# A fused transformer kernel in fp32: tiled score and compression matmuls, squares added on VectorE, a split GLU, and sparse attention ahead of latent attention

## The chip, the core and the metric

One core of one Trainium2 chip runs the whole program in one launch. The metric is device microseconds from the start to the end of an execution; the number compared is the median over several executions. The engines are named as in the profile: PE (TensorE matmul), PEld (its weight loads), DVE (VectorE), ACT (ScalarE), POOL (GpSimd) and SP (SyncE, which issues the weight loads from memory).

## The reference, cut to what matters

256 tokens of width 1024 go through one block of a first kind and then two layers of a second kind, all in fp32.

```python
def first_block(x, ...):
    xn = rms_norm(h, ln1_g)
    u_s5, q, k, v, gate_logits = split(xn @ w_in)
    y_s5 = s5_mixer(u_s5, ...) @ w_s5_branch      # scan, gelu, then ab = y @ w_glu; a * sigmoid(b)
    y_attn = sliding_window_attention(q, k, v, ...) @ w_attn_branch
    h = h + (g_s5 * y_s5 + g_attn * y_attn) @ w_out
    xn2 = rms_norm(h, ln2_g)
    return h + peer_mixer(xn2, w_query, sub_keys, u, v)   # s = q . sub_keys, top 16, 16384 experts

def layer(h):                                     # twice
    xn = rms_norm(h, attn_norm)
    q, k_cmp, v_cmp, k_sel, v_sel, k_win, v_win, gates, c_q, c_kv, k_rope = split(xn @ w_in)
    # NSA: compressed keys and values by a small MLP over blocks of 32 tokens (silu(flat @ w1) @ w2),
    # softmax over 15 compressed blocks, over the selected blocks and over the window; gated sum
    # MLA: q and k from normed c_q, c_kv; rotary part; softmax; values from c_kv
    h = h + concat(rms_norm(nsa), rms_norm(mla)) @ w_out
    xn = rms_norm(h, mlp_norm)
    return h + relu(xn @ w_ff1) ** 2 @ w_ff2
# at the end: rms_norm(h, final_norm)
```

## The kernel before, in words

Everything lies transposed: features on the 128 partitions, the 256 tokens along the free axis, so h is 8 chunks of 128x256. Weights come in units of 128x1024 fp32 (512 KB) in the order of use, through a ring of four SBUF slots that SP fills (L163 to L175, `Ring.load`).

**Split products.** Most products are made of three passes of fp32r matmuls: high part of the weights times high and low part of the data, low part of the weights times the high part. For each unit ACT rounds the weights to their high part (L177 to L185, `Ring.round`; two buffers `wh`, the next round waits until PE has finished the unit two before) and POOL subtracts to get the low part (L192 to L200, `Ring.subtract`). A slot is loaded again when POOL has made the low part (`rest`). `split_pair` (L1894) and `pair_product` (L516) take two units of 24 matmuls of 128x256 each. Other products are unsplit fp32 matmuls, which the trace records as two records each, and their slot comes free when PE has used it: `linear_part` (L364), `compress` (L2074), the scores (L1979), the sums of squares (L331 and L1883).

**PSUM** has 8 banks. `Banks.plan` (L95) gives each job its bank and its place in the order on that bank, by hand; `open` waits on PE until the job before it on the bank is drained, `take` waits on the reader until the job is full.

**The order of work on each engine is written out by hand**, an instruction stream per engine (`first_pe`, `first_act`, `first_dve`, and `layers_pe`, `layers_act`, `layers_dve`). Each engine takes its stream strictly in order; the position of a `ring.round` in ACT's stream is part of that order.

**The stretches of the program**, by the profile's times: the first block up to its last product (0 to 278.9 us) with the GLU inside (197.4 to 226.0), the two row products of the 16384 experts (to 1065), and twice a layer, made of its attention part (1068.9 to 1236.2 and 1429.0 to 1597.3) and its feed-forward part; the end is 1790.2 to 1804.0.

- In the first block PE makes `u` 0, then the sum of the squares of h by a matrix of ones over 8 chunks (L1173, L336), then `u` 1. ACT's stream is there: round, the eight high parts, round, the squares (L641), round, `table(0)` (sine and cosine tables, which wait for DVE's `angles(0)`, L827), round, the root of the mean square (L650).
- The GLU (L1245 to L1252) makes gb, ga and ys by 8 unsplit units.
- After `pq` (L1257 to L1261) and the first two expert rows, PE makes the 8 key score jobs of the experts (L2418 to L2426): 16 matmuls of 128x256 whose keys are padded with zeros to 128 rows. They use 4 banks, drained by ACT at L2243.
- In a layer PE does: cq, sum of 8 squares, ckr, q0, sum, turn, q1, the latent queries uq and keys uk and values uv (unsplit), the rotations rk and rq, kvc, latent scores (t = 0), rp, kk, latent scores (t = 1), rc, rp2, V, `compress` of the values (16 matmuls with 30 weight columns, L2080), the scores of the selected branch, `compress` of the keys, the scores of the window branch, then transposes and outputs of the latent heads, compressed scores sc, sum of 4 squares, the branch products wm, then (after a wait for the window probabilities and the compressed ones) transposes and outputs of the NSA heads, sum of 4 squares, branch products wn, and the feed-forward part with one more sum of 8 squares (mf). The keys KZ2 of the NSA scores are padded with zeros to 128 rows.
- DVE writes the scores with mask to SBUF (L1729), takes the row maximum (L1733, `row_max`), ACT makes the exponentials with their sums (L1552), DVE scales them by the reciprocal of the sum (L1742, `probabilities`). Rotations (`rope`, L1701) are PE, then three DVE instructions. The compressed scores are scaled, masked, shifted, normed in SBUF (L1807 to L1832).
- The end (L2192): sum of 8 squares after all four squares (L1646), root, reciprocal, scaling, store.

## Time and profile before

| | us |
|---|---|
| median of 3 executions | 1812.35 (1809.46 to 1813.52) |
| profiled execution, its own time | 1806.09 |
| its span in the profile | 1804.0 |
| mean granted TensorE clock | 0.987 of 2.4 GHz |
| PE busy / DVE / ACT / POOL | 95% / 49% / 51% / 66% |

The span is from the first to the last instruction of the profiled execution; 2.1 us of its own time lie outside. Busy time of PE counts a matmul from its start to its modelled end, so neighbours overlap: what one matmul costs in a row of equal ones is read from start to start. A fp32 matmul has two records.

### The profile page before, as it was taken

Reading aid. Unit: us, or ns where it says so; the run is one execution under the profiler, and the core shown is the slowest. Engines: PE = TensorE matmul, PEld = TensorE weight load, DVE = VectorE, ACT = ScalarE, POOL = GpSimd, SP = SyncE. Lnnn points to the kernel's source line nnn. Section 1 sums busy time; section 2 is a strip of 40 time slices with the busy share of each in tenths; the row PEclk is TensorE's granted clock in tenths of the full one; section 3 lists DMA queues with packets and bytes.
Section 4 is the critical chain, followed back from the end, with each engine's and each line's share of the span. In section 5 each row is a group of like instructions: output and inputs, shape, how many; then the busy total and the mean of one; then the engine's idle time right before and its main releaser. Section 6 shows DMA issues by size and latency. Waiting matters only on the chain.

```text
span 1804.0 us, 31918 instructions
## 1 busy us (share of the span) xinstructions
PE 1706.8 (95%) x12716; PEld 1545.4 (86%) x12716; DVE 875.9 (49%) x1854; ACT 912.1 (51%) x1530; POOL 1186.9 (66%) x492
## 2 busy tenths in 40 slices
PE   7988999989999999999999999988999989889997
PEld 7886899989999997777788887678999976789997
DVE  6978336991266666777511124853210148532101
ACT  5566355444544444555566664564653444646532
POOL 5552277898777776777788874215888741158885
PEclk9989999999999999999999999999999999899999
DMA  7332554655555554555566644413556543135563
GB/s 239 127 117 60 173 167 153 190 150 181 169 166 167 168 167 152 167 173 167 183 195 194 193 153 149 133 44 108 185 186 187 166 141 129 46 107 186 187 187 106
DMA packets 79603, 280.42 MB, mean 155 GB/s; under 512 B 8672, under 2 KB 9440, under 8 KB 79200
## 3 DMA queue, kind: packets, MB, share of 16 engines
q1 hardware_dynamic: 79456, 278.38, 49.3%
q8 instruction: 101, 1.65, 0.4%
q14 instruction: 46, 0.38, 0.1%
HBM read 277.30 MB, written 1.05 MB: 154 GB/s over the span
## 4 chain that ended last, share of the span: by engine, by line
PE 63%; DVE 5%; ACT 2%; issue 2%; POOL 1%; POOLq 0%; DVEq 0%; ACTq 0%
PE ps L2471 13%; PE ps L1903 13%; PE ps L2173 9%; PE ps L2478 6%; PE ps L2451 4%; PE ps L2452 3%; PE ps L2456 3%; ACT attention L1552 1%; POOL wl L199 1%; DVE attention L1729 1%; PE ps L1889 1%; PE ps L2437 1%; PE ps L1959 1%; PE ps L2439 1%; PE ps L2080 1%
## 5 line engine op out<-in xcount | busy, mean ns | idle before, releaser
L199 POOL TENSOR_TENSOR wl<-slots,wh 128x1024 fp32r<-128x1024 f32 x228 | 546.8, 2402 | 448.7 <-ACT wh L184 441.4
L2276 POOL TENSOR_TENSOR wl<-slots,wh 128x1024 fp32r<-128x1024 f32 x256 | 635.3, 2485 | 150.9 <-ACT wh L2216 148.8
L2216 ACT ACTIVATE wh<-slots 128x1024 fp32r<-128x1024 f32 x256 | 271.3, 1060 | 391.5 <-issue 234.3
L184 ACT ACTIVATE wh<-slots 128x1024 fp32r<-128x1024 f32 x228 | 240.5, 1060 | 263.0 <-PE ps L2173 105.5
L2451 PE MATMUL ps<-xh,wh 128*128 128x256 f32 x1024 | 255.9, 288 | 0.9 <-ACT small L2252 0.9
L2452 PE MATMUL ps<-xl,wh 128*128 128x256 f32 x1024 | 250.4, 282 | 0.0
L2451 PEld LDWEIGHTS ps<-xh,wh 128*128 128x128 f32 x1024 | 195.4, 191 | 1.1 <-ACT small L2252 1.1
L2452 PEld LDWEIGHTS ps<-xl,wh 128*128 128x128 f32 x1024 | 195.9, 191 | 0.0
L2471 PE MATMUL ps<-wh,xh 128*128 128x512 f32 x512 | 164.5, 403 | 4.4 <-DVE xl L2390 4.4
L2471 PE MATMUL ps<-wh,xl 128*128 128x512 f32 x512 | 160.0, 394 | 0.0
L2456 PE MATMUL ps<-xh,wl 128*128 128x256 f32 x1024 | 144.3, 284 | 7.9 <-POOL wl L2276 7.8
L2456 PEld LDWEIGHTS ps<-xh,wl 128*128 128x128 f32 x1024 | 131.9, 192 | 9.7 <-POOL wl L2276 9.7
L2478 PE MATMUL ps<-wl,xh 128*128 128x512 f32 x512 | 137.6, 391 | 0.0
L2173 PE MATMUL ps<-hidden_hi,wh 128*128 128x256 f32 x512 | 124.3, 280 | 1.9 <-POOL wl L199 1.9
L2390 DVE TENSOR_TENSOR xl<-ps,xh 128x256 fp32r<-128x256 f32 x128 | 53.7, 419 | 145.2 <-ACT xh L2231 145.2
L2173 PE MATMUL ps<-hidden_lo,wh 128*128 128x256 f32 x512 | 124.0, 279 | 0.0
L2478 PEld LDWEIGHTS ps<-wl,xh 128*128 128x128 f32 x512 | 96.4, 188 | 21.4
L2471 PEld LDWEIGHTS ps<-wh,xl 128*128 128x128 f32 x512 | 96.6, 189 | 21.0
L1903 PE MATMUL ps<-xh,wh 128*128 128x256 f32 x704 | 106.7, 291 | 6.9 <-ACT wh L184 4.6
L2383 DVE SCALAR_TENSOR_TENSOR arena<-ps,arena 128x256 f32<-128x256 f32 x128 | 54.4, 425 | 118.6 <-PE ps L2439 118.6
L2471 PEld LDWEIGHTS ps<-wh,xh 128*128 128x128 f32 x512 | 91.6, 189 | 20.6 <-issue 4.6
L1903 PEld LDWEIGHTS ps<-xh,wh 128*128 128x128 f32 x704 | 93.0, 193 | 13.6 <-issue 8.2
(357 smaller groups left out, 3204.6 us busy)
## 6 DMA issues: line engine op xcount, KB each, us to landing
slots<-w SPq DMA_DIRECT2D x260, 512.0 KB, 3.5
slots<-wu SPq DMA_DIRECT2D x128, 512.0 KB, 3.5
slots<-wv SPq DMA_DIRECT2D x128, 512.0 KB, 3.5
arena<-bias SPq DMA_DIRECT2D x1, 2048.0 KB, 8.1
h<-xT SPq DMA_DIRECT2D x2, 512.0 KB, 5.5
...
yT<-y_out SPq DMA_DIRECT2D x2, 512.0 KB, 2.6
...
```

Of the source, the lines that this page charges most:

```text
L184: act.activation(self.hi[:, n % 2, :], self.slots[:, u % SLOTS, :], ACT.Copy).then_inc(self.rounded, 1)
L199: pool.tensor_tensor(self.lo[:, n % 2, :], self.slots[:, self.order[n] % SLOTS, :], self.hi[:, n % 2, :].bitcast(F32), ALU.subtract).then_ ...
L1903: ins = pe.matmul(halves[j], w[:, k, :], x[:, k, :], start=(first and k == 0), stop=(last and k == DC - 1), skip_group_check=True)
L2173: return pe.matmul(out_banks[c // 2][:, (c % 2) * T:(c % 2 + 1) * T], w[:, c * P:(c + 1) * P], x[:, u, :], start=start, stop=False, skip_g ...
L2216: act.activation(whv[:, r % 2, :], slots_v[:, r % SLOTS, :], ACT.Copy).then_inc(w_hi, 1)
L2276: pool.tensor_tensor(wlv[:, r % 2, :], slots_v[:, r % SLOTS, :], whv[:, r % 2, :].bitcast(F32), ALU.subtract).then_inc(w_lo, 1)
L2383: dve.scalar_tensor_tensor(a, grid, 1.0 / GATE_SCALE, a, ALU.mult, ALU.mult).then_inc(g_done, 1)
L2451: pe.matmul(out, hi[:, k, :], xhT[:, k, :], start=(k == 0), stop=False)
L2452: ins = pe.matmul(out, hi[:, k, :], xlT[:, k, :], start=False, stop=False)
L2456: ins = pe.matmul(out, lo[:, k, :], xhT[:, k, :], start=False, stop=(k == DC - 1))
L2471: ins = pe.matmul(psum[2 * t + half], part_a[:, tokens], hi[:, half * 512:(half + 1) * 512], start=begins, stop=False, skip_group_check=True)
L2478: ins = pe.matmul(psum[2 * t + half], a_hi[:, t * P:(t + 1) * P], lo[:, half * 512:(half + 1) * 512], start=False, stop=(row == NE2 - 1), ...
```

## The change

What it does, part by part:

- **Added squares.** `add_squares` adds the chunks of squares on DVE (a reduction over a strided view), so that PE sums one matmul for each group of chunks: 1 for 8 in the first block (ms), 2 for 8 in ms2, ms and mf, 1 for 4 in mm and mn. At the end the 8 chunks stay, each pair awaited by itself.
- **Split GLU.** gb, ga and ys become split products (`split_linear`); ACT makes u_hi and glu_hi and rounds 8 more units, POOL subtracts 8 more, DVE makes u_lo and glu_lo.
- **Tiled key scores** of the experts: 32 matmuls of 64 rows and 128 columns, in pairs on the two row halves, two banks open at a time.
- **Tiled NSA scores**, in the same manner: for each group and t 8 matmuls of 64 rows in 4 pairs in place of 4 of 128 rows and twice the columns.
- **Tiled compression**: four matmuls with 32 weight columns each side by side in the four column groups, then ACT copies the 128 rows, and one more matmul by a matrix that adds the four tiles (`add_tiles`).
- **Compressed scores in PSUM**: their chain on DVE and ACT works in the bank of sc; only the finished probabilities go to SBUF.
- **The order of a layer**: rotations behind each product, NSA first, latent attention after it, wn before wm; the order of loads, rounds and banks with it. The NSA transposes use 3 banks in place of 7, the latent scores 2 in place of 4.

```diff
+        def add_squares(dve, squares, slot, signal):
+            dve.tensor_reduce(added[:, slot, :], squares.rearrange("p c t -> p t c"), AX.X, ALU.add).then_inc(signal, 1)
...
+        u_hi, u_lo, glu_hi, glu_lo = mix_hi[:, 0:4], mix_hi[:, 4:8], mix_lo[:, 0:4], mix_lo[:, 4:8]
...
@@ first_act, after the Gelu activations
+            act.wait_ge(s_gelu, UC)
+            act.activation(u_hi, uT, ACT.Copy).then_inc(s_uhi, 1)
+            ring.round(act, 2)
             for i in range(2):
                 b = banks.take(act, ("gb", i))
                 banks.give(act.activation(sig[:, 2 * i:2 * i + 2, :], two(b[:, :]), ACT.Sigmoid), ("gb", i))
+                ring.round(act, 1)
+            for i in range(2):
+                act.wait_ge(s_glu, i + 1)
+                b = banks.tensors[banks.jobs[("ga", i)][0]]
+                act.activation(glu_hi[:, 2 * i:2 * i + 2, :], two(b[:, :]), ACT.Copy).then_inc(s_ghi, 1)
+                ring.round(act, 1)
+            ring.round(act, 2)
...
@@ first_dve, ahead of angles(0)
+            dve.wait_ge(s_sq, 1)
+            add_squares(dve, sq, 0, s_pre)
             dve.wait_ge(loaded_c, 16)
             angles(0, early(0))
...
-            sum_squares(pe, "ms", sq, DC, (s_sq, 1))
+            sum_squares(pe, "ms", added, 1, (s_pre, 1))
...
-                    linear_part(pe, (name, i), ring.unit(pe).rearrange("p (k n) -> p k n", k=4), uT, (0, P))
+                    split_linear((name, i), u_hi, u_lo, lambda: pe.wait_ge(s_ulo, 1))
...
-            sum_squares(pe, "ms2", sq4, DC, (s_sq4, 4))
+            sum_squares(pe, "ms2", added, 2, (s_pre, 3))
...
@@ layers_act, from the root of msn on
+                copy(("kk", l), raw_k)
                 ring.round(act, 2)
                 b = banks.take(act, ("kvc", l))
                 act.activation(raw_c[:, 0, :], b[:, 0:T], ACT.Copy).then_inc(l_raw, 1)
                 ring.round(act, 1)
+                copy(("q", l, 1), raw_q[:, 2:4, :])
+                ring.round(act, 2)
+                copy(("cv", l), hidden_rows[:, 1, :])
+                exponentials(0, SELECTED, 0)
...
+                copy(("ck", l), hidden_rows[:, 0, :])
+                exponentials(0, SELECTED, 1)
...
+                for i in range(2):
+                    copy(("uq", l, i), qMr[:, 2 * i:2 * i + 2, :])
+                exponentials(1, WINDOW, 0)
...
+                for t in range(TT):
+                    copy(("uv", l, t), Vm[:, t, :])
+                exponentials(1, WINDOW, 1)
...
                 ring.round(act, 2)
...
+                exponentials(2, MLA, 0)
+                exponentials(2, MLA, 1, range(4))
+                ring.round(act, 1)
+                exponentials(2, MLA, 1, range(4, 8))
+                ring.round(act, 1)
+                banks.give(take_root(("mn", l), 512, root[:, 0:T]), ("mn", l))
                 transposed(16)
                 transposed(17)
...
@@ layers_dve
+                rope(("rp", l, 0), raw_q[:, 0:2, :], cos_r, sinr, add_to(qA[:, 0:2, :]))
                 banks.give(two_shifts(1, b[:, T:2 * T], rst[:, 0:T], ALU.mult), ("kvc", l))
                 windows(1)
                 rope(("rp", l, 2), raw_k, cos_r, sinr, split_keys)
+                rope(("rp", l, 1), raw_q[:, 2:4, :], cos_r, sinr, add_to(qA[:, 2:4, :]))
+                row_max(SELECTED, 0)
+                rope(("rc", l), raw_c, cos_r, sinr, lambda x, y: two_shifts(0, x[:, 0, :], y[:, 0, :], ALU.add))
+                windows(0)
+                row_max(SELECTED, 1)
+                projected_keys(0)
+                projected_keys(1)
+                row_max(WINDOW, 0)
+                projected_keys(2)
+                projected_keys(3)
                 for t in range(TT):
+                    probabilities(0, SELECTED, t)
                 row_max(WINDOW, 1)
...
+                probabilities(1, WINDOW, 0)
...
+                probabilities(1, WINDOW, 1)
...
-                link(dve.tensor_scalar(stc[:, 1], stc[:, 1], 1e-30, None, ALU.max))
-                link(dve.reciprocal(stc[:, 2], stc[:, 1]))
-                link(dve.tensor_tensor(stc[:, 2], stc[:, 2], GA[:, :, :, 0], ALU.mult))
+                link(dve.tensor_scalar(sums_c[:, 1], sums_c[:, 1], 1e-30, None, ALU.max))
+                link(dve.reciprocal(sums_c[:, 0], sums_c[:, 1]))
+                link(dve.tensor_tensor(stc[:, 1], sums_c[:, 0], GA[:, :, :, 0], ALU.mult))
+                for i in range(4):
+                    rope(("rq", l, i), qMr[:, 2 * i:2 * i + 2, :], cos_b, sin_b, add_to(qM[:, 2 * i:2 * i + 2, :]))
+                for c in range(2):
+                    mix_low(c, p2(l, "nsa")[:, c:c + 1])
+                row_max(MLA, 0)
+                for c in range(2, 4):
+                    mix_low(c, p2(l, "nsa")[:, c:c + 1])
+                row_max(MLA, 1)
+                dve.wait_ge(m_sq, 8 * l + 4)
+                add_squares(dve, squares_out[0], 0, l_pre)
...
@@ layers_pe
+                for g in range(2):
+                    both = [banks.open(pe, ("s", l, t, first + v)) for v in range(2)]
+                    for i in range(2):
+                        for v in range(2):
+                            rows = slice(64 * v, 64 * v + 64)
+                            ins = pe.matmul(both[v][:, i * w:(i + 1) * w], qA[rows, 2 * g + i, t * P:(t + 1) * P],
+                                            KZ2[rows, group, g, v, 0:w], start=True, stop=True,
...
+                        for n in range(4):
+                            ins = pe.matmul(bank[32 * n:32 * n + 32, 0:T], X[:, k, 4 * quarter + n, :], w[:, n, :],
+                                            start=(quarter == 0), stop=(quarter == 3), skip_group_check=True)
...
+                split_pair(("kk", l))
+                rotate(("rp", l, 0), "rot64", raw_q[:, 0:2, :])
+                split_pair(("kvc", l))
+                rotate(("rp", l, 2), "rot64", raw_k)
                 split_pair(("q", l, 1))
+                compress(("cv", l), 1, (0, 1))
+                rotate(("rc", l), "rot64", raw_c)
+                rotate(("rp", l, 1), "rot64", raw_q[:, 2:4, :])
+                compress(("cv", l), 1, (2, 3))
+                scores(SELECTED, 0)
+                values(("V", l))
+                scores(SELECTED, 1)
+                compress(("ck", l), 0, range(4))
+                latent_keys(w, 0)
+                latent_keys(w, 1)
+                scores(WINDOW, 0)
+                latent_keys(w, 2)
+                latent_keys(w, 3)
+                add_tiles(("cvs", l), 1, ("cv", l))
+                add_tiles(("cks", l), 0, ("ck", l))
+                latent_queries(0)
...
+                scores(WINDOW, 1)
+                latent_queries(1)
...
+                for i in range(3):
+                    turn_queries(i)
+                pe.wait_ge(l_prob, 6 * l + 4)
                 for c in range(5):
                     if c < 4:
+                        for hd in nsa_heads[c]:
+                            transposes(hd)
...
+                    if c == 4:
+                        latent_scores(0, True)
+                latent_scores(1, False)
+                for i in range(4):
+                    branch(("wn", l, i), l, 0, i == 0)
+                    if i == 0:
+                        sums(("mn", l), (0,), added, ready=(l_pre, 6 * l + 3))
+                pe.wait_ge(l_prob, 6 * l + 6)
...
-            sums(("end", 0), range(DC), sq, ready=(h_sq, 8 * LAYERS + 4))
+            for c in range(DC):
+                pe.wait_ge(h_sq, 8 * LAYERS + c // 2 + 1)
...
+                for n in range(4):
+                    hd = 4 * m + n
+                    for k in range(2):
+                        rows = slice(64 * k, 64 * k + 64)
+                        ins = pe.matmul(both[k][:, n * P:(n + 1) * P], qp[rows, hd, t * P:(t + 1) * P],
+                                        keys_v[rows, hd, k * P:(k + 1) * P], start=True, stop=True,
```

## Rows read from the trace of the kernel before

**Rows 1.** The page: busy time of each engine, with its share of the span.
```profile
PE 1706.8 (95%) x12716; PEld 1545.4 (86%) x12716; DVE 875.9 (49%) x1854; ACT 912.1 (51%) x1530; POOL 1186.9 (66%) x492
```

**Rows 2.** Busy time by stretch: span, PE, PEld, DVE, ACT, POOL, clock, DMA share, GB/s.
```profile
1068.91:1236.21 167.30, 151.11 (x1000) 123.97 (x1001) 97.93 (x152) 90.46 (x217) 54.87 (x23) 0.98 0.32 102
1429.01:1597.26 168.25, 152.97 (x1003) 126.06 (x1001) 97.34 (x151) 88.72 (x215) 51.27 (x22) 0.96 0.33 104
1193.60:1198.00 4.40, 4.32 (x25) 4.21 (x26) 4.30 (x4) 0.88 (x1) 4.39 (x2) 0.67 0.14 44
```

**Rows 3.** What PE waited for: us in total, times, longest.
```profile
PE ps L2154 <- DVE h L1846: 6.4, 2, 3.6
PE ps L1959 <- ACT wh L184: 6.4, 2, 3.2
```

**Rows 4.** Groups of PE by line: busy us, mean ns of a record.
```profile
L1889 PE MATMUL ps<-attention,cst 128*128 128x256 f32 x124 | 29.0, 383 | 4.4 <-DVE mix_lo L1771 2.9 <-ACT attention L1646 1.5
L2080 PE MATMUL ps<-slots,attention 128*30 128x256 f32 x128 | 28.4, 380 | 0.0
L370 PE MATMUL ps<-arena,slots 128*128 128x256 f32 x128 | 28.0, 380 | 0.8 <-issue 0.8
L1987 PE MATMUL ps<-layer,attention 128*128 128x256 f32 (+1 forms) x64 | 22.2, 495 | 2.7 <-DVE attention L1729 2.7
L1132 PE MATMUL ps<-arena 128*32 128x256 f32 x128 | 7.7, 382 | 0.6 <-DVE arena L889 0.6
L2424 PE MATMUL ps<-arena 128*128 128x256 f32 x32 | 7.1, 379 | 0.0
```

**Rows 5.** PE in order of time, start, us: paired tiles; a sum and its follower.
```profile
96.29 2.00 PE L1145 MATMUL ps<-arena 64*128 64x256 f32 x16
...
1076.38 3.62 PE L1889 MATMUL ps<-attention,cst 128*128 128x256 f32 x16
1079.64 1.30 PE L1903 MATMUL ps<-xh,wh 128*128 128x256 f32 x8
```

**Rows 6.** Groups of DVE by line, kept apart by shape: busy us, mean ns.
```profile
L2336 DVE TENSOR_TENSOR arena<-arena 128x2048 f32<-128x2048 f32 x4 | 17.4, 4359 | 0.1
...
L1742 DVE TENSOR_TENSOR attention<-attention,small 128x2048 f32<-128x2048 f32 x6 | 13.7, 2291 | 0.2
L1733 DVE TENSOR_REDUCE small<-attention 128x8 f32<-128x2048 f32 x6 | 13.7, 2286 | 0.2
...
L1733 DVE TENSOR_REDUCE small<-attention 128x8 f32<-128x1024 f32 x6 | 7.3, 1220 | 0.2
...
L1711 DVE TENSOR_TENSOR attention<-attention,ps 128x512 f32<-128x512 f32 x12 | 8.3, 688 | 0.4
...
L1830 DVE TENSOR_TENSOR small<-small,attention 128x16 f32<-128x16 f32 x2 | 4.0, 2014 | 0.1
```

**Rows 7.** The page: low parts of a unit, mean ns; a load's landing, us.
```profile
L199 POOL TENSOR_TENSOR wl<-slots,wh 128x1024 fp32r<-128x1024 f32 x228 | 546.8, 2402 | 448.7 <-ACT wh L184 441.4
...
slots<-w SPq DMA_DIRECT2D x260, 512.0 KB, 3.5
```

**Rows 8.** The start, in order of time: DVE, ACT, PE.
```profile
19.28 1.65 DVE L804 SCALAR_TENSOR_TENSOR arena<-cst,small,ps 128x256 f32<-128x256 f32 x4
...
24.12 1.04 ACT L184 ACTIVATE wh<-slots 128x1024 fp32r<-128x1024 f32 x1
...
25.21 1.22 PE L528 MATMUL ps<-xh,wh 128*128 128x256 f32 x8
```

**Rows 9.** Around the GLU, in order of time: the last Gelu; PE behind it.
```profile
193.76 1.34 ACT L759 ACTIVATE arena<-arena 128x256 f32<-128x256 f32 x4
...
228.43 0.50 PE L528 MATMUL ps<-xh,wh 128*128 128x256 f32 x2 [1.51 <-ACT xh L766]
```

**Rows 10.** ACT drains the first four key score banks.
```profile
287.66 2.09 ACT L2243 ACTIVATE arena<-ps 128x512 f32<-128x512 f32 x4
```

**Rows 11.** The end: PE's last sum.
```profile
1791.72 3.69 PE L1889 MATMUL ps<-attention,cst 128*128 128x256 f32 x16 [1.51 <-ACT attention L1646]
```

527 lines of the change are left out of this document (270 added, 257 removed).

## The prediction

> **What bounds it now.** I read the page's busy shares first, then PE's groups by line and its waits, then the timelines of PE, DVE, ACT and POOL around every stretch that the diff touches. PE is busy for 1706.8 us of the span of 1804.0, POOL for 66% [rows 1]: PE is the bound, and the waits are few. They lie in the two attention parts, of 167.30 and 168.25 us, of which PE is busy for 151.11 and 152.97 [rows 2]: 16.2 and 15.3 us of waits. The longest are for DVE ahead of the NSA heads (3.6) and for rounded weights behind the window exponentials (3.2) [rows 3]. After the latter the granted clock of 4.4 us was 0.67 [rows 2], between the levels 2.4 and 1.2 GHz; the same happens behind the other wait. At full clock this piece is 4.4 x 0.67 = 2.9 us, so each such dip costs 1.5 us; I count two a layer. The long expert rows, some 770 us, are untouched.
>
> So two things count: how much PE work goes away, and whether the new order hides DVE's and ACT's chains as well as the old one.
>
> **Prices.** An unsplit matmul of 256 columns is two records. `compress` has 64 of them in 28.4 us, 0.44 each; the S5 outputs, 64 matmuls of 32 columns of weights in four column groups, take 7.7 us, 0.12 each [rows 4]: the four do run side by side. 8 matmuls of a sum take 1079.64 - 1076.38 = 3.26 us, 0.41 each [rows 5]. Paired row halves: 8 matmuls of 256 columns in 2.00 us [rows 5], 0.50 a pair, half of that with 128 columns. A reduction over 2048 elements is 2.29 us, over 1024 1.22; any 512-element step 0.69 [rows 6]. The low part of a unit is 2.40, a load 3.5 [rows 7], rounding 1.04 [rows 8]. No row has a reduction with a strided input and 256 outputs. From below it costs what the same count costs there (1.22 for 1024), from above twice that; I take the low end, as the engine's rows go by elements. Doubling would cost 2.3 more at the start and under 1 in each sum elsewhere, where cover is 1 us or less: 7 us in all.
>
> The Trainium skill, TensorEngine Tiling (Array Packing), Key Properties, says that changing the tiling mode drains TensorE, which speaks against many short tiled groups; it states no time. The 64 column tiles above came in four groups, the 8 pairs in one, so what entering costs is in part in their prices; without it a pair would be 0.41, as one matmul of a sum, instead of 0.50.
>
> **First block.**
> - ms: 7 matmuls fewer, 2.9 us of PE. But DVE's reduction (2.3 us over 8 chunks) stands ahead of `angles(0)`, which ends at 19.28 + 1.65 = 20.9; `table(0)` follows on ACT and only behind it the next round, at 24.12, on which PE's second unit of `u` 1 starts at 25.21 with hardly a wait [rows 8]. All this comes 2.3 us later; the gain on PE turns into a wait of some 5 us, long enough for a clock dip. **+3.3**, between +2.3 (no dip) and +4.5.
> - GLU: 64 unsplit matmuls in 28.0 us [rows 4] become 192 at 0.12, 23. The last Gelu ends at 195.1 [rows 9], and PE is busy with ya 3 until 197.4, so u_hi (1.1) and the first round (1.1) are just ready; the first low part comes at 199.8, PE wants it at 199.3. After that a unit takes PE 2.9 against 1.1 + 2.4 for ACT and POOL, two buffers deep. glu_hi waits for ga 1, sigmoid and product: ys starts at 210.9, ends at 222.4, and the last of mixed_hi is at 224.4 where it was 228.43 [rows 9]. **-4.0**, between -5 and -1 (a late round shows at once).
> - ms2: 6 matmuls fewer; both reductions lie in gaps of DVE of 2 us. **-2.5**.
> - Key scores: 16 matmuls in 7.1 us [rows 4] become 16 pairs, 4.0. ACT drains the first four banks from 287.66 to 289.75 [rows 10] whatever PE does, so the second half waits for banks: **-1.6**. The rest of ACT's queue there is early by as much.
>
> **A layer's attention part**, PE work: sums 8 to 2, 4 to 1, 4 to 1, 12 x 0.41 = 4.9. Compression 14.2 to 32 x 0.12 plus two matmuls for the tiles (0.9), 9.4. Scores 11.1 to 8 x 0.50 + 8 x 0.25 = 6.0, 5.1. Together 19.4.
>
> Waits in the new order, laid out step by step from the start of cq at these prices (us, layer 0):
> - low part of ckr, behind POOL's memset, as ms now ends 2.4 earlier: 1.6 (layer 1: 0.4).
> - selected scores behind the three-step rope of q1: 2.1.
> - V, whose slot comes free only with `compress`: load, round, low part is 3.5 + 1.0 + 2.4 against five short jobs: 0.5.
> - uk, loaded into the slot of the first ck unit, which PE now needs for 2 us only: 2.1.
> - cks, its bank is uk 2's, which DVE drains behind `row_max(WINDOW, 0)`: 1.3.
> - the window probabilities. DVE's maximum comes when hT is over, ACT's eight exponentials behind the uv copies (some 4 us), then DVE's 2.29. PE has done sc and three rotations by then: 3.0, and 1.1 more for the compressed ones. Their chain in PSUM saves two steps that took 2.0 each for 16 elements [rows 6].
> - NSA heads on three banks 0.9; latent scores on two 0.7; mn, whose squares are added behind `row_max(MLA, 1)`, 1.4.
> - latent heads: ACT has 8 transposes, 8 steps of outputs and two rounds, 8.8, against 5.8 of PE: 3.0; then 1.1 to wm.
>
> That is 18.8, and one dip (1.5). The scaling of probabilities has two SBUF inputs: without POOL at work 2048 elements took 2.29 (L1742), beside POOL's steady low parts 4.36 (L2336) [rows 6]. In the new order two of them fall beside low parts of wn: I take 1.5 a layer, between 0 and 4. The Trainium skill, GPSIMD Engine Reference, Specifications, says that GpSimd's SBUF interfaces are shared with VectorE for instructions with two SBUF inputs; these two rows agree. So the new waits and dips are 21.8, the old ones 16.2 + 3.0 = 19.2. Gain 19.4 - 2.6 = 16.8 by this ledger; laying the steps end to end gives 19 to 20 instead, because my list counts overlapping waits twice. I take **-18.5**, and **-20.5** for layer 1 (no memset, and its old dips are longer).
>
> The loads are no bound: the DMA share there is 0.33 [rows 2].
>
> **Feed-forward, end.** mf: 6 matmuls fewer, twice, and the root on which ACT's rounds wait comes as much earlier: **-5.0**. End: the sum started at 1791.72 after a wait for all squares [rows 11]; by pairs it starts at 1790.2 and stays PE-bound: **-1.6**.
>
> **Sum.** +3.3 - 4.0 - 2.5 - 1.6 - 18.5 - 20.5 - 5.0 - 1.6 = -50.4. The profiled execution took 1806.1 (2.1 outside its span) and would take 1755.7; it lies 6.3 below the median of the executions, 1812.35, so the median becomes **1762**.
>
> **Rivals.**
> - *DVE keeps ahead* (0.25). The waits that hang on DVE's queue (q1's rope, cks, window probabilities, mn: 8.9) and the 3.0 of dip and contention go: 24 us less, **1738**. For it: DVE is busy for only 98 of 167 us [rows 2]. Against: its work is in chains, one after the other.
> - *DVE or ACT falls behind* (0.15). The new order puts three softmaxes on one queue with the ropes; if each hand-over costs 1 us more than the bare durations, 9 a layer: **1780**.
> - *The clock* (0.04), the one that ends slower. More short tiles with waits between them make PE less busy in the attention parts, and the granted clock stays at its lower level for longer. Its place is the stretch from `compress` of the keys to the latent heads. With 2 x 128 us of PE work, the gain of 50 is gone when 256 x (1/c - 1) = 50, at a granted clock of 0.84 (before 0.98 and 0.96 [rows 2]). At 0.75 it is **1847**. Against: the short transposes there run at full clock today.
> - *The tiles don't overlap* (0.03): compression and scores cost as before, +20.6 + 10.2 + 2.4: **1795**. Against: the two tiled rows above.
> - Forecast (0.53), its own range 1748 to 1774.
>
> **Numbers.** 1738 to 1786 leaves out the clock, the failed tiles, and the far ends of the others, some 2 in 10. An effect of 0.2% (3.6 us) is about what a measurement of this kernel can tell. All cases but the clock are faster by over 0.2%: 0.95; within 0.2%: 0.01; slower: 0.04.
>
> **What would show it.** In the profile after: the squares' sums at 2 records each in the first block; u 1's second unit at about 27.5 with a wait for ACT's round; `compress` at about 2 us for 16 matmuls; out 0 some 1 us earlier than before; attention parts of about 148 us with clock above 0.94; waits of PE for DVE's probabilities of about 3 us and for a load of uk. Wrong would be: attention parts under 137 or over 158 us, a start that gains, a reduction that takes over 1.5 us for 1024 elements, or a granted clock under 0.9 there.

## The result, and the profile after

The changed kernel takes 1755.8 us (median of 4 runs, 1755.4 to 1756.2), the kernel before 1810.9 (median of 4, 1807.8 to 1813.5): ratio 0.9711 as recorded, 95% interval 0.9692 to 0.9731 (the two medians by themselves divide to 0.9696). The forecast ratio was 1762 / 1812.35 = 0.9722. Between the two profiled executions the span goes from 1804.0 to 1753.6 us, 50.4 less, which is the forecast sum to the digit. The medians lie 55.1 apart, because the profiled execution of before was 4.8 us faster than its own median and that of after only 0.4. That it agrees so closely is luck: some single terms missed by more than the sum did, and they cancelled. A second profiled execution of the changed kernel (e12) has the same span of 1753.6 us with its parts distributed otherwise: its first GLU matmul starts at 198.01 us in the place of 200.73, and its expert rows take 3.1 us more.

The page of the changed kernel, busy times of the engines (its counterpart is [rows 1]):

```profile
PE 1656.9 (94%) x12786; PEld 1509.6 (86%) x12786; DVE 910.8 (52%) x1875; ACT 919.0 (52%) x1541; POOL 1210.7 (69%) x500
```

PE has 49.9 us less to do, DVE 34.9 more. PE's share hardly moved, though the waits in the attention parts did. The two attention parts of the changed kernel, by the view of busy time by stretch (columns as in [rows 2]: span, PE, PEld, DVE, ACT, POOL, clock, DMA share, GB/s), and the places with a clock dip in layer 0:

```profile
1063.51:1212.34 148.83, 137.21 (x1013) 114.67 (x1013) 105.56 (x158) 89.21 (x217) 56.63 (x23) 0.97 0.35 114
1402.54:1551.12 148.58, 136.19 (x1015) 113.70 (x1014) 104.69 (x156) 87.25 (x215) 53.93 (x22) 0.97 0.36 119
1066.20:1071.50 5.30, 5.30 (x33) 5.30 (x33) 5.30 (x8) 5.25 (x10) 4.50 (x2) 0.68 0.16 41
1151.40:1155.30 3.90, 3.85 (x20) 3.03 (x20) 3.66 (x12) 2.58 (x6) 3.90 (x2) 0.56 0.13 17
1181.40:1186.00 4.60, 4.60 (x26) 4.55 (x26) 2.73 (x3) 2.77 (x9) 2.38 (x1) 0.63 0.06 15
```

Against [rows 2] the parts are 18.5 and 19.7 us shorter (forecast 18.5 and 20.5); waits of PE fell from 16.2 to 11.6 in layer 0, where the forecast had them rise a little. What PE waits for between the start of layer 0 and the end of the attention part of layer 1, in total, times, longest (compare [rows 3]):

```profile
PE ps L421 <- issue: 6.1, 2, 3.1
PE ps L1990 <- DVE small L389: 5.6, 5, 2.1
PE ps L2190 <- issue: 4.8, 2, 2.4
PE ps L2126 <- DVE mix_lo L1846: 2.9, 4, 0.7
PE ps L2096 <- issue: 2.5, 2, 1.2
```

"issue" means that the profile names no releaser; what these waits are for is read from the order of the code, and e8 and e11 test two of them. L421 is the first transposed NSA head, behind the window probabilities; L1990 a sum of squares behind DVE's addition (L389); L2190 the latent keys, behind the load of uk; L2096 the selected scores behind the rope; L2126 the outputs of the latent heads. They are the waits that the ledger named. By stage, between the profiled executions (the marks are PE's first matmul of each stage):

| stage | before, us | after, us | change | forecast |
|---|---|---|---|---|
| start to the first GLU matmul | 197.35 | 200.73 | +3.4 | +3.3 |
| GLU, to the low weights of out 0 | 31.42 | 27.81 | -3.6 | -4.0 |
| out 0 to the expert rows (ms2) | 50.12 | 47.92 | -2.2 | -2.5 |
| expert rows (key scores) | 787.93 | 784.96 | -3.0 | -1.6 |
| attention part, layer 0 | 167.30 | 148.83 | -18.5 | -18.5 |
| feed-forward, layer 0 | 192.80 | 190.20 | -2.6 | -2.5 |
| attention part, layer 1 | 168.25 | 148.58 | -19.7 | -20.5 |
| feed-forward, layer 1, to the last sum | 194.46 | 190.18 | -4.3 | -4.1 |

The 16 transposes between the expert rows and layer 0, 2.1 us from start to start in both kernels, stand in no row. The last row is the second mf together with the wait of 1.51 ahead of the last sum [rows 11], now gone. Of the 3.0 in the expert rows 1.4 are the key scores themselves (6.7 us before, 5.3 after). The rest lies in a part that the change doesn't touch: where the up rows give way to the down rows, the granted clock of before was 0.83 for 10 us and that of after 1.00. Busy time of the stretch from 690 to 700 us (columns as above), of the kernel before and of the changed one:

```profile
690.00:700.00 10.00, 10.00 (x51) 7.78 (x50) 6.04 (x15) 4.03 (x8) 4.77 (x2) 0.83 0.33 106
```

```profile
690.00:700.00 10.00, 10.00 (x65) 7.77 (x64) 7.74 (x21) 5.01 (x9) 7.94 (x4) 1.00 0.44 129
```

The changed kernel's second profiled execution (e12) has 788.1 for the stage, with a granted clock of 0.93 from 665 to 690 us, where the first has 1.00. So such a dip comes and goes between executions of one kernel, and nothing here ties it to the change.

The start, in order of time (start, us): DVE, ACT and PE, for comparison with [rows 8], and the additions outside ms2 by form (ns, min/median/max):

```profile
16.23 3.77 DVE L389 TENSOR_REDUCE small<-attention 128x256 f32<-128x2048 f32 x1
...
27.70 1.04 ACT L184 ACTIVATE wh<-slots 128x1024 fp32r<-128x1024 f32 x1
...
20.15 0.67 PE L337 MATMUL ps<-small,cst 128*128 128x256 f32 x2 [1.49 <-DVE small L389]
...
28.79 2.08 PE L535 MATMUL ps<-xh,wh 128*128 128x256 f32 x8 [5.11 <-ACT wh L184]
...
L389 DVE TENSOR_REDUCE small<-attention x13: 1937/2028/3775, 16.2 to 1557.8; 128x256 f32<-128x1024 f32 x12, 128x256 f32<-128x2048 f32 x1
```

PE's second unit of u 1 starts at 28.8 us, not at 25.2, behind ACT's rounding, which is queued behind the sine table, which waits for DVE's angles, which stand behind the addition. The 8 matmuls take 2.08 us there in the place of 1.22 [rows 8]: a clock dip behind a wait of 5.1 us. The addition with its strided input takes 3.78 us for 2048 elements and 2.0 for 1024; reductions along the row took 2.29 and 1.22 [rows 6].

### The profile page after: what moved, and what is told of

Read it like the earlier page. It is cut to its first block, busy times and chain, and to the rows that moved or that the text cites. A ratio compares the mean times of both kernels' runs of the same rounds, so it can differ in the third digit from the quotient of the medians.

```text
span 1753.6 us, 32136 instructions
## 1 busy us (share of the span) xinstructions
PE 1656.9 (94%) x12786; PEld 1509.6 (86%) x12786; DVE 910.8 (52%) x1875; ACT 919.0 (52%) x1541; POOL 1210.7 (69%) x500
## 4 chain that ended last, share of the span: by engine, by line
PE 64%; DVE 3%; issue 2%; POOL 1%; ACT 1%; POOLq 0%; DVEq 0%; ACTq 0%
PE ps L2608 14%; PE ps L2004 12%; PE ps L2302 10%; PE ps L2615 7%; PE ps L2588 4%; PE ps L2589 3%; PE ps L2593 3%; POOL wl L199 1%; PE ps L2060 1%; PE ps L2574 1%; PE ps L2576 1%; PE ps L370 1%; PE ps L2126 1%; PE ps L2072 1%; PE ps L2065 1%
## 5 line engine op out<-in xcount | busy, mean ns | idle before, releaser
L199 POOL TENSOR_TENSOR wl<-slots,wh 128x1024 fp32r<-128x1024 f32 x236 | 570.7, 2421 | 379.1 <-ACT wh L184 363.1
L2410 POOL TENSOR_TENSOR wl<-slots,wh 128x1024 fp32r<-128x1024 f32 x256 | 635.3, 2485 | 147.9 <-ACT wh L2349 145.8
L2349 ACT ACTIVATE wh<-slots 128x1024 fp32r<-128x1024 f32 x256 | 271.3, 1060 | 389.6 <-issue 235.3
L184 ACT ACTIVATE wh<-slots 128x1024 fp32r<-128x1024 f32 x236 | 249.4, 1060 | 262.1 <-PE ps L2302 105.5
L2608 PEld LDWEIGHTS ps<-wh,xh 128*128 128x128 f32 x512 | 91.4, 189 | 20.5 <-issue 4.6
```

What stands on the lines that cost most here:

```text
L184: act.activation(self.hi[:, n % 2, :], self.slots[:, u % SLOTS, :], ACT.Copy).then_inc(self.rounded, 1)
L199: pool.tensor_tensor(self.lo[:, n % 2, :], self.slots[:, self.order[n] % SLOTS, :], self.hi[:, n % 2, :].bitcast(F32), ALU.subtract).then_ ...
L2349: act.activation(whv[:, r % 2, :], slots_v[:, r % SLOTS, :], ACT.Copy).then_inc(w_hi, 1)
L2410: pool.tensor_tensor(wlv[:, r % 2, :], slots_v[:, r % SLOTS, :], whv[:, r % 2, :].bitcast(F32), ALU.subtract).then_inc(w_lo, 1)
L2608: ins = pe.matmul(psum[2 * t + half], part_a[:, tokens], hi[:, half * 512:(half + 1) * 512], start=begins, stop=False, skip_group_check=True)
```

## The experiments

All were timed beside the kernel before, in three groups on three chips: e1 to e4, e5 to e8, and e9 to e12. The kernel before had medians of 1809.3, 1805.1 and 1807.0 us beside them, and 1810.9 beside the changed kernel. So medians of different groups can lie some 5 us apart with nothing changed, and the ratios are the safer comparison across them. Parts are layer 0 / layer 1 of the profiled execution.

| run | median, us (range) | ratio to before, 95% | attention parts, us |
|---|---|---|---|
| e1 old order, new arithmetic | 1796.3 (1792.7 to 1799.1) | 0.9935, 0.9915 to 0.9956 | 165.7 / 168.0 |
| e9 the same, tile sums later | 1802.5 (1800.6 to 1806.7) | 0.9970, 0.9956 to 0.9984 | 170.9 / 171.2 |
| e2 sums alone | 1796.2 (1795.7 to 1797.8) | 0.9931, 0.9912 to 0.9950 | 168.1 / 167.4 |
| e3 GLU alone | 1804.2 (1801.5 to 1807.3) | 0.9976, 0.9963 to 0.9990 | 169.4 / 168.3 |
| e4 full rows | 1764.1 (1763.0 to 1765.7) | 0.9755, 0.9736 to 0.9774 | 152.2 / 152.4 |
| e5 tree of additions | 1753.1 (1751.3 to 1756.3) | 0.9712, 0.9696 to 0.9728 | 147.0 / 146.5 |
| e6 rounds first | 1749.0 (1748.2 to 1752.7) | 0.9692, 0.9676 to 0.9708 | 149.8 / 147.6 |
| e7 ms by PE | 1752.1 (1750.4 to 1754.5) | 0.9701, 0.9685 to 0.9717 | 150.0 / 147.6 |
| e8 selected later | 1756.6 (1756.0 to 1760.0) | 0.9735, 0.9719 to 0.9751 | 149.2 / 147.8 |
| e10 e5 and e6 | 1750.2 (1743.4 to 1754.6) | 0.9676, 0.9649 to 0.9704 | 149.5 / 145.7 |
| e11 e10, heads early | 1751.7 (1748.6 to 1752.9) | 0.9688, 0.9671 to 0.9704 | 148.1 / 148.0 |
| e12 changed kernel again | 1755.6 (1755.2 to 1761.5) | 0.9720, 0.9702 to 0.9739 | 149.1 / 147.8 |

### Is it the arithmetic or the order? (e1, e9)

The forecast counted PE work that goes away (19.4 us a layer) and asked whether the new order hides DVE and ACT as well as the old one did. The opposite question, what the arithmetic is worth in the old order, tests what the order is for.

```diff
-                            ins = pe.matmul(bank[0:30, 0:T], X[:, k, 4 * quarter + n, 0:30], w[:, n, :],
-                                            start=(quarter + n == 0), stop=(quarter + n == 6))
+                            ins = pe.matmul(bank[32 * n:32 * n + 32, 0:T], X[:, k, 4 * quarter + n, :], w[:, n, :],
+                                            start=(quarter == 0), stop=(quarter == 3), skip_group_check=True)
...
-                scores(SELECTED, 0)
-                scores(SELECTED, 1)
+                tiled_scores(SELECTED, 0)
+                tiled_scores(SELECTED, 1)
                 compress(("ck", l), 0)
-                scores(WINDOW, 0)
-                scores(WINDOW, 1)
+                tiled_scores(WINDOW, 0)
...
+                add_tiles(("cvs", l), 1, ("cv", l))
+                add_tiles(("cks", l), 0, ("ck", l))
+                tiled_scores(WINDOW, 1)
```

The kernel is the one before with these lines and those of the diff outside the layers; `tiled_scores` is the changed kernel's `scores`.

> The kernel before, with all the new arithmetic (split GLU, squares added on DVE at the start and for ms2, ms and mf, row-tiled key scores and NSA scores, column-tiled compression with the sum over the tiles, the sum at the end by pairs), but with latent attention ahead of NSA as before, and with the norms of the two branches (mm, mn) summed by four matmuls each as before. The change's own stages outside the attention parts are then +3.4, -3.9, -1.9, -1.4, 2 x -2.6 and -1.5 = -10.5 against the kernel before; the attention parts lose sums 3.3 (one of 8 to 2 at 0.41, less what DVE delays), compression 8.9 and NSA scores 4.8 of PE work, 16.2 each. Theory (the order is worth little, the arithmetic nearly all): attention parts of 167.3 - 16.2 = about 151 to 153, the whole about 1763 to 1768 us. Rival (the old order can't use the tiles: its waits for DVE and for loads grow by what PE gives back): attention parts of 158 or more, the whole 1775 us or more.

Measured: 1796.3 us, a span of 1790.9, 13.1 under that of before, of which 11.2 lie outside the attention parts. The attention parts are 165.7 and 168.0: nearly all of the 16 us of PE work a layer was lost again. In layer 0 PE's busy time fell by 11.4 us only (from 151.1 to 139.7, for part of what is left runs at the lower clock), and its waits grew by 9.8 (from 16.2 to 26.0). The rival is right, and by more than it said. PE of this kernel in layer 0, in order of time, and busy time by stretch over the same work, of this kernel and then of the kernel before (columns as above):

```profile
1144.87 1.23 PE L2073 MATMUL ps<-layer,attention 64*128 64x128 f32 x16 [2.03 <-issue]
1149.53 3.53 PE L2073 MATMUL ps<-layer,attention 64*128 64x256 f32 x16 [3.43 <-DVE attention L1796]
...
1161.17 1.03 PE L2082 MATMUL ps<-attention,small 128*32 128x256 f32 x2 [4.61 <-ACT attention L1555]
1164.33 3.79 PE L2073 MATMUL ps<-layer,attention 64*128 64x256 f32 x16 [2.14 <-DVE attention L1796]
...
1140.90:1169.44 28.54, 16.34 (x140) 11.10 (x140) 24.31 (x35) 13.10 (x44) 4.67 (x2) 0.71 0.46 166
```

```profile
1145.82:1172.09 26.27, 24.94 (x98) 12.72 (x98) 23.22 (x34) 14.65 (x43) 3.99 (x2) 1.00 0.50 163
```

The stretch runs from the compression of the values to the head of the latent transposes. Before, PE was busy for 24.9 of its 26.3 us and DVE for 23.2: two engines nearly full side by side, and the view of PE's waits showed only one of them. With the tiles PE has 16.3 us, lower clock included, and DVE still 24.3. The stretch is 28.5 us long, and with these gaps PE's granted clock is 0.71. DVE is not all of it: it has 4.2 us of gaps there, and PE's wait of 4.61 is for ACT, which makes 16 exponentials (1151.3 to 1160.7) ahead of its copy of the keys' tiles.

> The old order with the new arithmetic again, but with the sums over the compression's tiles behind the window scores, in the place of between their halves, where PE waited 4.6 us a layer for ACT to drain the keys' tiles. Theory (DVE's chain of maxima and probabilities sets this stretch in the old order, PE's work no longer does: DVE works from 1144.7 to 1171.7 with 3.8 us of gaps): the second half of the window scores still waits for DVE's banks until about 1163.5, a layer gains 1 to 1.5, about 1794 us. Rival (my place for the two sums made the old order look bad): 4 us a layer and more, 1788 us or under.

```diff
-    add_tiles(("cvs", l), 1, ("cv", l))
-    add_tiles(("cks", l), 0, ("ck", l))
     tiled_scores(WINDOW, 1)
+    add_tiles(("cvs", l), 1, ("cv", l))
+    add_tiles(("cks", l), 0, ("ck", l))
```

Measured: 1802.5 us, parts of 170.9 and 171.2. PE and ACT of this kernel in layer 0, in order of time:

```profile
1165.91 3.52 PE L2073 MATMUL ps<-layer,attention 64*128 64x256 f32 x16 [7.94 <-DVE attention L1796]
...
1170.02 0.80 ACT L1639 ACTIVATE attention<-ps 30x256 f32<-30x256 f32 x2 [6.11 <-PE ps L2082]
```

As the theory said, the second half of the window scores still waits for DVE, now for 7.9 us in one piece. The gain of 1 to 1.5 was wrong: ACT stands for 6.1 us ahead of its Silu, with the rounded weights and the transposed heads queued behind it, and a layer loses 3 to 5. The rival falls as far as this one other place can show. Both placements stay 40 us and more above the changed kernel. Of that, 2 x 3 x 0.41 = 2.5 a layer is work (mm and mn are still 4 matmuls each here); the rest of the 17 and 19 us a layer is the order and what goes with it (kept in one block: the place of each branch, the plan of the banks, the chain of compressed scores in PSUM, ACT's copies). Those were not taken apart, and no run has the new order with the old products. So it is shown that the new products gain almost nothing in the old order; that the order alone gains nothing is not shown.

### The parts alone (e2, e3, e4)

> The kernel before with one part of the change alone: the squares of ms2, of the layers' ms and of mf are added on DVE in two halves and summed over the partitions by 2 matmuls in the place of 8. Theory: each of the five sums gives 6 x 0.41 = 2.5 us of PE, DVE's two steps of 2.0 lie in its gaps: 12 us less, about 1799 us. Rival (DVE's steps are late): the two layers' ms show waits of PE for the addition of 1 us and more, 8 us less or under.

```diff
-                sums(("ms", l), range(DC), sq, ready=(h_sq, 8 * l + 4))
+                sums(("ms", l), range(2), added, ready=(l_pre, 4 * l + 2))
...
-                        sums(("mf", l), range(DC), sq, ready=(h_sq, 8 * l + 8))
+                        sums(("mf", l), range(2), added, ready=(l_pre, 4 * l + 4))
```

Measured: 13.1 us less by the medians, 9.3 by the spans; by stage 2.5 (ms2), 2.6 and 2.6 (feed-forward), but nothing that can be seen in the attention parts (168.1 / 167.4 against 167.3 / 168.3, that of layer 0 at a granted clock of 0.96 against 0.98). The two ms wait for the addition (PE in total, times, longest):

```profile
PE ps L1906 <- DVE small L389: 2.0, 2, 1.0
```

So the rival has the ms right: of 2.5 us, 1.0 goes to waiting for the slow addition, and the 1.5 that should be left can't be told from the scatter of the parts. The medians' 13.1 and the spans' 9.3 frame the sum of 12.

> The kernel before with the split GLU alone. Theory: as in the whole change, where the stretch from the first gate matmul to the last high part of the mixed rows went from 31.1 to 27.2 us: 3.9 us less, the stretch 27.2 here too. Rival (that gain came from the start being late, so that ACT and POOL were ahead when the GLU began): 2 us less or under, with waits of PE for rounded or low parts inside it.

```diff
-                    linear_part(pe, (name, i), ring.unit(pe).rearrange("p (k n) -> p k n", k=4), uT, (0, P))
+                    split_linear((name, i), u_hi, u_lo, lambda: pe.wait_ge(s_ulo, 1))
...
-                linear_part(pe, ("ys", i), ring.unit(pe).rearrange("p (k n) -> p k n", k=4), gluT, (0, P))
+                split_linear(("ys", i), glu_hi, glu_lo, glu_low_ready)
```

Measured: the stretch from the first GLU matmul to the low weights of out 0 is 27.8 us here and 27.8 in the changed kernel, against 31.4 before: 3.6 less. The whole is 5.1 us less (ratio 0.9976, 0.9963 to 0.9990). The start is the old one here, so the rival falls. The waits inside are the same as in the changed kernel, 0.35 for the first low part and 1.47 for the rounded GLU rows:

```profile
197.26 1.21 PE L1180 MATMUL ps<-mix_hi,wl 128*128 128x256 f32 x8 [0.35 <-POOL wl L199]
...
208.42 2.11 PE L1175 MATMUL ps<-mix_lo,wh 128*128 128x256 f32 x16 [1.47 <-ACT mix_lo L777]
```

> The changed kernel with its NSA scores over all 128 rows (the other half of the keys is zero) in the place of pairs of 64 rows side by side: each matmul runs alone. The pairs take 1.16 us a bank pair set of 128 columns and 2.00 of 256; alone they should take 2 x 0.94 = 1.9 and 2 x 1.9 = 3.8 or a little under. Theory (the pairs' gain is real PE time on the path): 2 x (0.8 + 1.7) = 5 us more a layer, less what existing waits of 1.2 and 2.4 take up: 8 to 10 us more, about 1765 us. Rival (ACT's and DVE's chains set the pace of the attention part): under 4 us more.

```diff
-    rows = slice(64 * v, 64 * v + 64)
+    rows = slice(0, 128)
```

Measured: 1764.1 us, 8.3 more by the medians and 7.7 by the spans, parts of 152.2 and 152.4 (+3.4 and +3.8). PE's group of NSA scores in layer 0, over all rows:

```profile
L2096 PE MATMUL ps<-layer,attention 128*128 128x128 f32 (+1 forms) x64 | 12.1, 348 | 1.2 <-issue 1.2
```

By rows it was 6.3 us: the pairs do run side by side, and undone they put 5.8 us on PE. In the new order that shows as 3.4 to 3.8, where in the old one (e1) all the tiles together showed as 1.6 and 0.2. The theory stands, but not its reason for the rest: the waits for the rope (1.2), for uk (2.6) and for the window probabilities (3.1) are as long as before. What is smaller is what the clock took: from 1145 to 1160 and from 1176 to 1190 us the granted clock is 1.00 here, 0.89 and 0.88 in the changed kernel, so two dips of some 1.7 us didn't fall behind the same two waits. Another one fell at the wait for uk instead (granted clock 0.79 from 1127 to 1135 us), where it costs less: the latent keys behind it take 4.7 us in the place of 4.0. PE's busy time rose by 2.8 in all (140.05 against 137.21) and its waits by 0.5. Why the dips moved is open.

### The start (e6, e7) and the addition (e5)

> The changed kernel with its first sum of squares as before: 8 matmuls on PE, no addition on DVE ahead of the angles. Theory: the second half of u 1 starts at 25.2 us again, and the start's loss of 3.4 us is undone: about 1752.4 us. Rival (the loss comes from something else at the start): within 1 us of 1755.8.

```diff
-    add_squares(dve, sq, 0, s_pre)
-    sum_squares(pe, "ms", added, 1, (s_pre, 1))
+    sum_squares(pe, "ms", sq, DC, (s_sq, 1))
```

Measured: 1752.1 us, u 1's second unit at 25.3, 3.5 us earlier. The theory holds for this unit and, by the median, for the whole. The ratio alone (0.9701, 0.9685 to 0.9717) can't tell the kernel from the changed one (0.9711 and 0.9720), and in the profiled execution the first GLU matmul starts at 197.9, 0.1 us ahead of that of e12, whose first matmul of all came 1.4 us earlier. The nearest kernel of the same group with the late start is e8, with 1756.6.

> The changed kernel with ACT's order at the start changed: the rounding of the second half of u 1, the root of ms and one more rounding stand ahead of the first sine table, in the place of behind it. Theory (PE's wait of 5.1 us there hangs on ACT's queue being held by the table, which waits for DVE's angles, which stand behind the addition): the second half of u 1 starts at about 24 us, the wait is gone or 1 to 2 us of it come back at k; 3 to 5 us less, about 1751.5 us. Rival (the same wait reappears at k, since its rounding now stands behind the table): under 1 us less.

```diff
-    table(0)
     ring.round(act, 1)
     b = banks.take(act, "ms")
...
-    ring.round(act, 3)
+    ring.round(act, 1)
+    table(0)
+    ring.round(act, 2)
```

Measured: 1749.0 us (ratio 0.9692, 0.9676 to 0.9708), the lowest median of all; 3.1 less than e7 and 7.5 less than e8 in the same group, 6.7 less than the changed kernel's own median in another. By the ratios the gain over the changed kernel is 3.4 to 5 us. The wait is gone, the first GLU matmul starts at 195.0, and what comes behind the old place of the wait is 0.4 and 0.3 us:

```profile
23.40 1.12 PE L535 MATMUL ps<-xh,wh 128*128 128x256 f32 x8
...
26.84 1.21 PE L535 MATMUL ps<-xh,wh 128*128 128x256 f32 x8 [0.40 <-DVE arena L853]
...
32.59 1.22 PE L535 MATMUL ps<-xh,wl 128*128 128x256 f32 x8 [0.32 <-POOL wl L199]
```

> The changed kernel with the squares added by plain additions of halves (1024 elements: one step of 512 outputs and one of 256; 2048 elements: 1024, 512, 256) in the place of the reduction with a strided input, which took 1.94 to 2.03 us for 1024 elements and 3.78 for 2048, where a reduction along the row took 1.22 and 2.29. Theory (the stride makes the reduction slow): 0.69 + 0.42 = 1.1 and 1.2 + 1.1 = 2.3. The start comes 1.4 us earlier; PE's waits for the addition shrink by 0.9 each at mn, twice, and at mf of layer 1's ms by 1.0: 4 us less in all, about 1752 us. Rival (it is the arithmetic or contention, not the stride): the additions take as long, and the time stays at 1755.8.

```diff
-    dve.tensor_reduce(added[:, slot, :], squares.rearrange("p c t -> p t c"), AX.X, ALU.add)
+    while n > 1:
+        dve.tensor_tensor(squares[:, 0:n, :], squares[:, 0:n, :], squares[:, n:2 * n, :], ALU.add)
+        n //= 2
+    dve.tensor_tensor(added[:, slot, :], squares[:, 0, :], squares[:, 1, :], ALU.add)
```

Measured: 1753.1 us; attention parts of 147.0 and 146.5, waits for the addition 3.4 in the place of 5.6. The form of the reduction was the cost: where POOL is idle the same 1024 elements take 0.68 + 0.43 us. A gain in the whole is not shown: the ratio, 0.9712, is that of the changed kernel (0.9711 and 0.9720). Between single executions parts of the same code differ by 2 us, so the 1.8 and 2.1 less can be read only together; over the profiled executions with and without the tree (3 and 5) the mean part is 147.5 against 148.6. In these additions both inputs lie in SBUF, and beside POOL's low parts they are dear. Of the 14 additions of 1024 elements in e5 five meet one, and each of these takes 2.3 to 3.2 us in all, more than the reduction did. DVE of e5, the first additions of ms2 and of layer 0's ms (POOL's low parts end at 245.13 and 1071.29):

```profile
242.18 0.68 DVE L402 TENSOR_TENSOR arena<-arena 128x512 f32<-128x512 f32 x1
242.90 2.52 DVE L404 TENSOR_TENSOR small<-arena 128x256 f32<-128x256 f32 x1
...
1069.90 1.94 DVE L402 TENSOR_TENSOR attention<-attention 128x512 f32<-128x512 f32 x1
1071.88 0.43 DVE L404 TENSOR_TENSOR small<-attention 128x256 f32<-128x256 f32 x1
```

DVE of e5 and then of e10, the last step of the addition at the start, in order of time (in e5 POOL's low part starts at 18.55, just behind it; in e10 at 18.64, ahead of it):

```profile
18.48 0.43 DVE L404 TENSOR_TENSOR small<-attention 128x256 f32<-128x256 f32 x1
```

```profile
18.84 2.47 DVE L404 TENSOR_TENSOR small<-attention 128x256 f32<-128x256 f32 x1
```

A step of 0.43 us that starts 0.2 us after POOL's operation lasts about as long as POOL's whole operation (2.4). In the three slow places shown the step ends 0.3 to 0.6 us behind the end of POOL's low part (245.13, 1071.29 and, in e10, 21.02), wherever in it the step started; the one that started 0.07 us ahead of it isn't touched. That is the row behind the rule of the Trainium skill which the prediction quoted (GPSIMD Engine Reference, Specifications: SBUF interfaces shared for instructions with two SBUF inputs), and this trace agrees with it more sharply than [rows 6] did. The reduction has one input and hardly suffers from it: 1.94 to 2.08 wherever it stands.

### Two waits that the ledger named (e8, e11) and the sum of the gains (e10, e12)

> The changed kernel with one step of PE's order moved: the second half of the selected scores (2.0 us) behind the compression of the keys in the place of ahead of it. The compression frees its slots 2 us earlier, so the load of uk starts earlier and the scores lie beside it. Theory (PE's wait of 2.4 us ahead of uk is the load): the wait falls to about 0.4 and a layer gains 2.0, less 0.5 to 1 for the selected probabilities that come later on ACT's and DVE's queues: 2 to 4 us less, about 1752.5 us. Rival (DVE or ACT set the later steps anyway): the gain turns up as a longer wait for the window probabilities (3.1 now), and the time stays within 1 us.

```diff
-    scores(SELECTED, 1)
     compress(("ck", l), 0, range(4))
+    scores(SELECTED, 1)
```

Measured: 1756.6 us, no gain (ratio 0.9735, 0.9719 to 0.9751). The wait for uk's load is gone in layer 0; PE in order of time:

```profile
1124.14 1.99 PE L2190 MATMUL ps<-attention,slots 128*128 128x256 f32 x8
1126.07 1.16 PE L2096 MATMUL ps<-layer,attention 64*128 64x128 f32 x16
1127.16 1.13 PE L2190 MATMUL ps<-attention,slots 128*128 128x256 f32 x4
1128.84 1.13 PE L2190 MATMUL ps<-attention,slots 128*128 128x256 f32 x4 [0.55 <-DVE attention L1792]
...
1132.62 0.62 PE L2170 MATMUL ps<-attention,small 128*32 128x256 f32 x2 [2.10 <-DVE attention L1792]
```

It was the load, but the 2.4 us come back as 0.55 and 2.10 for DVE, which takes the latent keys out of their banks behind the later selected maxima. The rival is right in what it says of the time; the place is a bank, not the window probabilities (still 3.1).

The kernel e10 has the edits of e5 and e6 together, e11 one more, e12 is the changed kernel without an edit.

> The changed kernel with the two edits that gained: plain additions of halves, and two roundings and the root ahead of the first sine table. Theory: the roundings gave 6.0 us of span (4.5 to 6 at the start), the additions 1.7 at layer 0 and 2.0 at layer 1; at the start the addition now holds PE for 1.3 us only, which goes: about 1753.6 - 5.5 - 3.8 - 1 = 1743.5 of span, 1745 us. Rival (DVE's additions hold up the start elsewhere, beside POOL): no better than 1748.

> As the kernel with both edits, and the transposes of the first two selected heads stand ahead of PE's wait for the window probabilities. Theory (the wait of 3.1 us is for the last window probabilities alone, the selected ones are there 13 us before): PE does 0.7 us of work inside it, the wait is 2.4, a layer gains 0.7: 1 to 1.5 us less than the kernel with both edits. Rival (ACT's copies of the transposed heads, behind its own queue, set the pace behind the wait): no gain.

```diff
-                pe.wait_ge(l_prob, 6 * l + 4)
+                pe.wait_ge(l_prob, 6 * l + 2)
                 for c in range(5):
                     if c < 4:
-                        for hd in nsa_heads[c]:
+                        for n, hd in enumerate(nsa_heads[c]):
+                            if c == 0 and n == 2:
+                                pe.wait_ge(l_prob, 6 * l + 4)
                             transposes(hd)
```

> The changed kernel once more, beside the others on the same chip. Theory: its time is known, 1753.5 to 1756.5 us, and what it scatters by tells which of the small differences above can be read. If the first unit's arrival and the dips of the clock at the start scatter as in the other runs, single executions differ by up to 3 us; rival: within 0.5 us as in its first four.

Measured: 1750.2 us with both edits (1743.4 to 1754.6), 1751.7 with the third. Neither can be told from e6 alone: e10's ratio is a little lower (0.9676 against 0.9692), its median a little higher, and the intervals overlap. e10's theory gave 1745, and only 1743.4 and 1745.9 of its five runs are there. These two have a mean granted clock of 0.990, the two slowest (1753.8 and 1754.6) one of 0.984; by an estimate from these numbers, 0.006 of 1750 us is 10 us, about the spread of the five. At the start of the profiled one the tree's last step met POOL (2.47 above), and PE waited 2.2 us for the addition where e6 waits 1.3. Whether that has a part in the lower clock of the slower ones can't be seen, since one execution alone was profiled. In e11 the two early heads are transposed inside the wait, and what is left of it is two waits; PE in order of time:

```profile
1146.88 0.33 PE L436 MATMUL ps<-cst,attention 128*128 128x128 f32 x1 [2.36 <-DVE attention L1834]
...
1149.04 1.01 PE L2286 MATMUL ps<-cst,attention 128*15 128x128 f32 x4 [0.85 <-DVE attention L1925]
```

2.36 + 0.85 = 3.2 where there was 3.1: the compressed probabilities, next in DVE's queue, are now the late ones. The wait fell to 2.4 as the theory had it, and the time is the rival's (no gain), but for another reason than the rival's, ACT's copies. The changed kernel again has 1755.6, with one of five at 1761.5.

## Why the prediction was right, point by point

**The bound.** PE as the bound was half of it. The sentence "how much PE work goes away, and whether the new order hides DVE's and ACT's chains as well as the old one" named the right two things, but the ledger set the order's own worth at about nothing (new waits and dips 21.8 against 19.2). e1 and e9 show that this was only true with the order in place: the same tiles in the old order gain 2 us at most. [rows 1] and [rows 3] can't show that DVE is as full as PE where PE doesn't wait yet; a view of busy times of that stretch would have. That DVE's load is what made the old order lose is argued from these views; in e1 a wait for ACT of 4.6 us a layer has a part in it too.

**The attention part, -18.5.** PE's groups of layer 0 that the change touches (sums, compression with the two tile sums, NSA scores) had 14.2 + 11.1 + 9.0 = 34.3 us and have 4.1 + 1.2 + 6.3 + 2.4 + 1.5 = 15.5: 18.8 less, forecast 19.4. Without them and the dips PE's busy time rose by 2.8 us (latent scores 0.7, latent keys 0.4, queries 0.3, rotations 0.3 and smaller ones), not in the ledger. PE's groups of the changed kernel in the attention part of layer 0:

```profile
L2096 PE MATMUL ps<-layer,attention 64*128 64x128 f32 (+1 forms) x64 | 6.3, 336 | 1.2 <-issue 1.2
L2160 PE MATMUL ps<-slots,attention 128*32 128x256 f32 x64 | 4.1, 384 | 0.0
L1990 PE MATMUL ps<-small,cst 128*128 128x256 f32 x8 | 2.4, 398 | 2.3 <-DVE small L389 2.3
L2170 PE MATMUL ps<-attention,small 128*32 128x256 f32 x4 | 1.2, 391 | 0.4 <-DVE attention L1792 0.4
```

L2096 are the NSA scores, L2160 the compression: 64 records of 384 ns in 4.1 us, four side by side. The waits are 11.6, forecast 18.8. Those sized well: the window probabilities 3.1 (3.0), uk 2.4 (2.1). Too dear: the rope ahead of the selected scores 1.2 (2.1), cks 0.4 (1.3), the latent heads 1.7 (3.0) and then 0.2 (1.1), V 0.1 (0.5), the low part of ckr 0 (1.6), the NSA heads on three banks 0 (0.9), the latent scores on two 0 (0.7), and the compressed probabilities 0 (1.1), which are late only once the window's come earlier (e11: 0.85). Too cheap: mn 2.1 (1.4), for the addition is slow. The clock dips are three, not one: 5.30 x 0.32 + 3.90 x 0.44 + 4.60 x 0.37 = 5.1 us, forecast 1.5. The contention of the probabilities with POOL didn't come: 2.29 and 2.37 us a step, forecast 1.5 a layer more. Together -18.8 + 2.8 + (11.6 - 16.2) + (5.1 - 3.0) = -18.5. The ledger alone had -16.8; that laying the steps end to end gave 19 to 20 was the better half of the argument. So the term is right in what goes away, and its exact size is luck: waits that were 7.2 too dear stand against 3.6 of dips and 2.8 of busy time that were not foreseen.

**The start, +3.3.** Right in its chain, wrong in a price. The step that failed is "I take the low end, as the engine's rows go by elements": the strided reduction takes 3.78 us and not 2.3, 2.0 and not 1.22. So u 1's second unit came at 28.8, not at 27.5, by the condition named in the prediction ("a reduction that takes over 1.5 us for 1024 elements") a miss. The sum hid it, because small waits that stood behind the old place (0.30 and 0.61) went away and clock dips fell elsewhere; and the +3.4 is itself a reading of two single executions. The first GLU matmul of the kernels with the old start is at 197.35 (before), 195.71 (e2) and 194.86 us (e3), of those with the new start at 200.73 (the changed kernel), 198.01 (e12), 198.56 (e1), 198.43 (e9), 198.03 (e4) and 198.70 (e8): by the means the start costs 2.8. That 3.4 met 3.3 so closely is luck too; what does repeat is the wait of 5.11 us, in both executions of the changed kernel. The sign "out 0 some 1 us earlier" didn't come either: its first matmul starts at 226.13 where it was 225.97. e6, e7: the loss is the place of the addition in DVE's queue, and most of it was ACT's, to be had back by two roundings and a root that don't wait for the sine table.

**GLU, ms2, mf, end.** -3.6, -2.2, -2.6, -4.3 against -4.0, -2.5, -2.5 and -4.1: the prices of 0.12 and 0.41 carry over. e3 shows the GLU's alone. (A slip without effect: the 8 matmuls in 2.00 us are 4 pairs, as the price of 0.50 a pair has it, not the 8 pairs that the prediction speaks of beside the tiling mode.)

**Key scores, -1.6.** 1.4, with PE's predicted wait for ACT's banks (1.2); the other 1.6 of the stage is a clock dip of the execution before.

**The rivals.** "The tiles don't overlap" falls on the trace and on e4. "DVE or ACT falls behind" and "the clock" are both real, in the old order: e1 and e9 show waits for DVE of 11 and 23 us in two layers and a granted clock of 0.71 in the stretch. In the new order they stayed within the forecast. "DVE keeps ahead" didn't come: the waits for it are there.

**The median.** The forecast was 6.3 above the profiled execution's sum, since before's was that far below its median; after's is 0.4 below. In 13 runs the kernel before spread over 1804.2 to 1813.4. Of the 6.2 us by which the forecast of 1762 is above 1755.8, 5.9 are this offset and not the terms. The part of the forecast that rests on a single profiled execution is good to some 4 us in this kernel.
